# Loading the transposed input in eight pieces through a second DMA queue, in a hybrid encoder kernel

## The reference

```python
def ssd_mixer(u, in_proj, conv_w, conv_b, dt_bias, a_log, d_skip, norm_w, out_proj):
    zxbcdt = u @ in_proj                       # (256, 2048) @ (2048, 10368)
    z, xbc, dt_raw = ...                       # 4096, 6144 and 128 columns
    xbc = silu(centred_depthwise_conv(xbc, conv_w, conv_b))
    ...                                        # scan both ways, gate with silu(z), RMS norm
    return gy @ out_proj

def reference(x, ...):
    for i in range(DEPTH):
        x = layer_norm(ALPHA * x + mix(x), g, b)
        x = layer_norm(ALPHA * x + square(relu(x @ w1[i])) @ w2[i], g, b)
    return x
```

## Time and profile before

| | us |
|---|---|
| median of 3 runs | 2206.31 |
| lowest and highest | 2205.95, 2207.38 |
| the profiled execution | 2205.52 |
| its span | 2203.8 |

### The profile page before, as it was taken

The page is one execution under the profiler, slowest core; times in us unless marked ns, Lnnn a source line. Parts: engine busy times, 40 slices in busy tenths (PEclk is TensorE's granted clock), DMA queues, the critical chain, the costliest instruction groups (busy, mean ns, idle before and its releaser), DMA issues.

```text
span 2203.8 us, 31261 instructions
## 1 busy us (share of the span) xinstructions
PE 2163.3 (98%) x10626; PEld 1817.0 (82%) x10626; DVE 1439.6 (65%) x1778; ACT 1109.6 (50%) x1549; POOL 234.0 (11%) x172
## 2 busy tenths in 40 slices
PE   9999999999999999999999999989999999999997
PEld 7788888888887778888888888867888888888886
DVE  6787867858768855555565655696565655555656
ACT  5677747757665544444353443446343443443433
POOL 0213322303310500000000000033000000000001
PEclk9999999999999999999999999999999999999999
DMA  8969896988956665555555555446555555555553
GB/s 272 252 202 237 237 278 180 238 230 227 239 183 221 203 212 184 182 200 176 205 190 190 195 185 180 168 152 227 191 191 190 200 181 187 194 180 200 190 191 115
DMA packets 246963, 443.96 MB, mean 201 GB/s; under 512 B 14048, under 2 KB 49040, under 8 KB 245216
## 3 DMA queue, kind: packets, MB, share of 16 engines
q1 hardware_dynamic: 206608, 397.52, 53.8%
q0 software_dynamic: 35664, 28.66, 7.6%
q10 hardware_dynamic: 4608, 16.78, 2.0%
HBM read 440.68 MB, written 2.23 MB: 201 GB/s over the span
## 4 chain that ended last, share of the span: by engine, by line
PE 85%; DVE 7%; DMA 3%; ACT 2%; issue 2%; DVEq 0%; ACTq 0%; SPq 0%
PE acc L357 13%; PE acc L359 13%; PE acc L358 13%; PE acc L608 9%; PE acc L615 5%; PE tb L608 5%; PE sbk L608 5%; DVE wlo L1101 3%; PE sbk L359 3%; PE sbk L357 3%; PE tb L357 3%; PE tb L359 3%; PE tb L358 3%; PE sbk L358 3%; PE sbk L615 2%; PE tb L615 2%
## 5 line engine op out<-in xcount | busy, mean ns | idle before, releaser
L718 ACT CAST whi<-raw 128x1024 fp32r<-128x1024 f32 x746 | 774.8, 1054 | 672.2 <-DMA raw<-in_w 269.8
L1101 DVE TENSOR_TENSOR wlo<-raw,whi 128x1024 fp32r<-128x1024 f32 x746 | 920.4, 1271 | 195.9 <-ACT whi L718 191.4
L357 PE MATMUL acc<-whi,xT 128*128 128x512 f32 x800 | 322.0, 402 | 12.7 <-DVE wlo L1101 10.9
L359 PE MATMUL acc<-wlo,xT 128*128 128x512 f32 x800 | 312.8, 391 | 0.0
L358 PE MATMUL acc<-whi,xT 128*128 128x512 f32 x800 | 312.2, 390 | 0.0
L357 PE MATMUL acc<-whi,hTl 128*128 128x512 f32 x768 | 304.6, 397 | 6.0 <-DVE hTl L1121 3.3
L358 PE MATMUL acc<-whi,hTh 128*128 128x512 f32 x768 | 299.8, 390 | 0.0
L359 PE MATMUL acc<-wlo,hTh 128*128 128x512 f32 x768 | 299.8, 390 | 0.0
L608 PE MATMUL acc<-xT,whi 128*128 128x512 f32 x896 | 224.0, 392 | 0.0
L357 PEld LDWEIGHTS acc<-whi,xT 128*128 128x128 f32 x800 | 150.7, 188 | 49.0 <-issue 9.0
L608 PEld LDWEIGHTS acc<-xT,whi 128*128 128x128 f32 x896 | 162.0, 189 | 29.6
(11 more groups left out here) (207 smaller groups left out, 2675.0 us busy)
## 6 DMA issues: line engine op xcount, KB each, us to landing
raw<-in_w SPq DMA_DIRECT2D x512, 512.0 KB, 4.7
raw<-in_in_proj SPq DMA_DIRECT2D x162, 512.0 KB, 5.4
raw<-in_out_proj SPq DMA_DIRECT2D x64, 512.0 KB, 7.4
spare<-in_masks ACTq DMA_DIRECT2D x16, 512.0 KB, 7.4
spare<-f_scratch POOLq DMA_DIRECT2D x32, 256.0 KB, 15.4
area_d<-in_masks ACTq DMA_DIRECT2D x8, 512.0 KB, 5.9
area_d<-f_scratch POOLq DMA_DIRECT2D x16, 256.0 KB, 6.9
area_c<-in_masks ACTq DMA_DIRECT2D x8, 512.0 KB, 7.2
```

Of the source, the lines that this page charges most:

```text
L357: pe.matmul(dst, lhs[1][:, kt, rows(t)], hi, start=first and i == 0, stop=False)
L359: mm = pe.matmul(dst, lhs[0][:, kt, rows(t)], lo, start=False, stop=end)
L718: act.copy(whi[:, s.slot(RING)], raw[:, r]).then_inc(hi_ready, 1)
L1101: dve.tensor_tensor(wlo[:, slot], raw[:, r], whi[:, slot].bitcast(F32), ALU.subtract).then_inc(lo_ready, 1)
```

## The change

The transposed x is loaded in eight pieces of 256 KB (two k-steps, one weight tile's worth) in place of four of 512 KB. ACT issues them, through its own DMA queue: two ahead of everything, and piece c + 2 right after the cast of piece c. I call the pieces x0 to x7. SP's queue keeps the weights, the identity and later the rows of x. The casts on ACT, the remainders on DVE and the products on PE follow the eight pieces: piece c, then tile c.

```diff
-        xt_in = [sem(f"xt_in_part{c}") for c in range(4)]
+        xt_in = [sem(f"xt_in_part{c}") for c in range(8)]
...
-        xt_parts = a["xt"].rearrange("p (c k n) -> c p k n", c=4, k=CT)
+        xt_parts = a["xt"].rearrange("p (c k n) -> c p k n", c=8, k=SUBK)
...
-            for c in range(4):
-                sp.dma_start(xt_raw[:, CT * c:CT * (c + 1), :], xt_parts[c]).then_inc(xt_in[c], 16)
-                for i in (2 * c, 2 * c + 1):
-                    load(Pos(S_B0 + i), in_w[:, SUBK * i:SUBK * (i + 1), B0:B0 + NB])
+            load_in(Pos(S_B0), B0)
...
-            sp.wait_ge(xt_lo, 4)
+            sp.wait_ge(xt_lo, 8)
...
-                for c in range(4):
+                for c in range(8):
                     pe.wait_ge(xt_lo, c + 1)
                     for t in range(TT):
-                        products(xT, range(4 * c, 4 * c + 4), t, Pos(Q_B0), Pos(S_B0 + 2 * c), c == 0, c == 3)
+                        products(xT, range(SUBK * c, SUBK * (c + 1)), t, Pos(Q_B0), Pos(S_B0 + c), c == 0, c == 7)
...
-            for c in range(4):
+            def load_xt(c):
+                act.dma_start(xt_raw[:, SUBK * c:SUBK * (c + 1), :], xt_parts[c]).then_inc(xt_in[c], 16)
+            load_xt(0)
+            load_xt(1)
+            for c in range(8):
                 act.wait_ge(xt_in[c], 16)
-                act.copy(xT[0][:, CT * c:CT * (c + 1), :], xt_raw[:, CT * c:CT * (c + 1), :]).then_inc(xt_hi, 1)
-                split_hi(Pos(S_B0 + 2 * c))
-                split_hi(Pos(S_B0 + 2 * c + 1))
+                act.copy(xT[0][:, SUBK * c:SUBK * (c + 1), :], xt_raw[:, SUBK * c:SUBK * (c + 1), :]).then_inc(xt_hi, 1)
+                if c < 6:
+                    load_xt(c + 2)
+                split_hi(Pos(S_B0 + c))
...
-            for c in range(4):
-                part = (slice(None), slice(CT * c, CT * (c + 1)))
+            for c in range(8):
+                part = (slice(None), slice(SUBK * c, SUBK * (c + 1)))
                 dve.wait_ge(xt_hi, c + 1)
                 lo_of(xT[1][part], xt_raw[part], xT[0][part], xt_lo)
-                split_lo(Pos(S_B0 + 2 * c))
-                split_lo(Pos(S_B0 + 2 * c + 1))
+                split_lo(Pos(S_B0 + c))
```

## The result

The changed kernel takes 2209.19 us (median of 22 runs, 2204.67 to 2213.56), the kernel before 2205.53 us (median of 22 runs beside them, 2202.10 to 2209.51). The ratio is 1.0016 with a 95% interval of 1.0010 to 1.0022: by the ratio 3.5 us slower, between 2.2 and 4.9. That is inside the range of the forecast and on its side, but three times the +1.1 us. Ratios leave out single executions far from all others: one of 2395.65 us among the 11 of pieces_small_late, and one of 7741.91 us of the kernel before beside it.

What follows compares the result with a forecast made beforehand. The prediction took the path of weight tiles, DVE and ACT to bound the start, with PE busy behind it. PE's start swallowed, issues and splits 0, t17 +1.1 us: 2206.31 + 1.1 = 2207.4 us, range 2204.6 to 2210.2.

Steps and rivals of the forecast that it cites:

- What bounds the start: Up to 68 us: PE's own path has 2.66 us of slack; the path of tiles, DVE and ACT has none.
- Issues, and more but smaller operations: First group: ACT's added issues hidden beside casts, split casts (+0.6 us) and remainders (+0.3 us) in idle time; cost 0.
- Start of PE: First products: PE begins 0 to 0.7 us earlier than 9.13, which is swallowed by its later wait.
- A late piece: Forecast's mechanism: late x5 and x7 hold ACT's casts, DVE's remainders and SP's issues; t17 0.4 to 2.6 us late; chance 0.46.
- the sign: ACT's casts of x5 near 19.3 and x7 near 24.2 us show idle time put down to the DMA of x.
- L = 4.8 us: Time from a piece's issue on ACT's queue to its landing, taken as 4.8 us from the masks' loads.
- The third rival: Pieces on ACT's queue take over 6.5 us, making the kernel 4.4 us or more slower; chance 0.08 past 4.4 us.
- Shift of t17: Weight tile t17, which gates the convolution, lands 1.1 us late through t9 and t13, all of it passed on.
- From 68 us on nothing but the shift: Behind PE's idle times at 63 and 68 us, the rest of the kernel only moves by the start's delay.
- a sign of being wrong: Convolution starting before 44.3, pieces landing within 4 us, or PE's idle time after 68 us changing.
- Sum: Start of PE swallowed, issues and splits 0, shift of t17 +1.1 us: median 2206.31 + 1.1 = 2207.4 us.
- the forecast's own case: Late pieces delay t17 by 0.4 to 2.6 us, giving 2206.7 to 2208.9 us; chance 0.46.

Runs made afterwards that it cites:

- pieces_small_late: Kernel before with x in eight pieces, each issued from SP ahead of its tile, and POOL's seven small loads held back until t7 is done: 2204.71 us, ratio 0.9996.
- pieces_alone: Kernel before with x in eight pieces, each issued from SP's queue right ahead of its tile: 2204.90 us, ratio 1.0001.
- four_ahead: Changed kernel with four pieces asked for ahead of everything and piece c + 4 behind the cast of piece c: 2205.73 us, ratio 1.0004 to the kernel before.
- changed_again: Unchanged copy of the changed kernel, run at another time: 2208.47 us, ratio 1.0022 to the kernel before.
- small_loads_late_after: Changed kernel with POOL's seven small loads held back until eight remainders are done: 2207.44 us, ratio 1.0009 to the kernel before.
- queue_alone: Kernel before with x still in four parts, but issued through ACT's queue, two parts ahead: 2205.70 us, ratio 1.0006.
- all_ahead: Changed kernel with all eight pieces asked for at the start on ACT's queue: 2208.02 us in one run, ratio not timed.

## Why the prediction was right or wrong

- *What bounds the start.* Right: two paths, one of PE and one of tiles, DVE and ACT, and the time goes with the second. The shift of the convolution arrives at the turn in full.
- *Issues, and more but smaller operations, at nothing.* Right: pieces_alone makes all the smaller operations and eight issues on SP and has a ratio of 1.0001. ACT's issue rows in the changed kernel lie beside its casts.
- *Start of PE, 0 to 0.7 us earlier and swallowed.* The size was a little short (0.9), the rest right: the waits of 0.61 and 1.99 us in the first group took it back.
- *A late piece holds ACT, then DVE, then SP.* The mechanism is right: four_ahead removes ACT's waits for x and with them the loss. Its place is not: the late row is x2, x4, x6, and not x3, x5, x7. The schedule had t2 cast at 13.5 as before and never asked when x2, which now stands ahead of it, would land; x2 is cast at 13.80 and t2 at 14.33. The casts of x5 (20.66) and x7 (25.39), whose waits were to be the sign, have none.
- *L = 4.8 us.* This is the term that failed. The masks' times were turned into a piece's by giving each queue half of 385 GB/s. x2 and x3 took 8.9 and 9.2 us (7.9 and 7.9 in changed_again), x4 to x7 3.7 to 5.4. From x4 on the estimate was thus good; it fails for the two pieces that are asked for while four tiles stand on SP's queue. Half the rate is what x2 got once its packets ran; but in small_loads_late_after the first of them ran only about 3.5 us after the request (5.9 us in all), and the dip of the small loads puts 2 to 4 us on top. The prediction had seen the dip and its likely maker and given it no price. The third rival, which had L over 6.5 us for all pieces, comes nearer for x2 and x3, but its reason for doubt ("half as long as the masks") says nothing on the time ahead of the first packet.
- *Shift of t17: +1.1 us.* It measured +2.75 (44.89 against 42.14), and +3.2 over the repeated profiles.
- *From 68 us on nothing but the shift.* Wrong by 0.7: the prediction let PE's idle time at 63 us grow at no cost. It grew to 2.38 us only, and the lower clock behind it came on top. The prediction had named a change of PE's idle time after 68 us as a sign of being wrong, and there is one: the turn had 0.57 us ahead of it and has none now.
- *Sum.* 2.75 + 0.67 = 3.4 us from one pair of profiles, or 3.2 + 0.8 = 4.0 from the repeated ones, against 3.5 and 4.8 us in the ratios of the two timings (3.7 and 3.5 between the medians). The forecast's one term was mis-sized, and one term was missing. How much of it each part of the change makes can't be split finer than this: queue_alone, at 1.0006, is unclear.
- *The number.* That 2209.19 lies within the range owes something to luck. It is above the band of the forecast's own case (to 2208.9), in the stretch from 2.6 to 4.4 us late that was given a chance of 0.06. And the forecast stood on a median of three runs, 2206.31, that was 0.8 us above that of 22 (2205.53).

What stays open is the second drop of the DMA rate, at 15 to 22 us, in the kernels with x on ACT's queue. In the changed kernel little that had been asked for was left to move by 16 us, since ACT's two-deep window and SP's four tiles both wait on late casts. In small_loads_late_after, 4.7 MB had moved by 15.36 (307 GB/s), with more asked for than that, so a lack of requests doesn't explain it there.

## What to carry to other kernels

A load that is asked for on a second queue, while the first has a deep backlog, can land much later than its size or a share of the rate says: here its packets began 3.5 us after the request. Read that time from a trace before you choose how far ahead to ask. If its landing gates the engine that also frees the backlog's slots, give it as many requests ahead as the other queue has (four here, not two), or leave it in the one queue in the order of use. And when a change lengthens an idle time of PE that is "slack", look at the granted clock behind it before you cost it at nothing.

## What the runs showed of the hardware

- 256 KB asked for at 4.86 us on ACT's queue with the engines full landed 5.9 us later, after 2.3 MB had moved (small_loads_late_after). Its queue moved nothing from 6.50 to 8.30 us; from 8.50 to 10.50 us both queues moved the same, 0.39 and 0.38 MB.
- With pieces always waiting on ACT's queue, the two queues moved 0.61 and 0.58 MB from 12 to 15 us (all_ahead), and a piece overtook a tile that had been asked for 1.2 us earlier.
- Seven small loads of POOL, 0.21 MB in all, coincide with 2.5 us (7.5 to 10) at 78 to 238 GB/s in the middle of a stream of 375 to 396, and without them the dip is gone. By these rates they cost the stream some 0.6 MB, an estimate, about three times their bytes.
- Idle times of PE of 2.38 to 3.17 us ahead of t18 were followed by a granted clock of 0.5 and cost 0.7 to 0.9 us; those of 0.36 to 2.13 us were not. At the first products, idle times of 1.99 us were followed by the lower clock and one of 2.06 us was not.
- The start of the convolution in one kernel varies by 1.5 to 2.6 us from one profiled execution to the next.
